# A wider column pitch for the split activations of a decoder-layer kernel, with small tiles placed in the gaps

## What is computed

```python
x = x + 0.5 * swiglu_ffn(x, ffn1_norm, ffn1_w_in, ffn1_w_out)   # 1024 -> 2 x 2816 -> 1024
h = rmsnorm(x, mix_norm); proj = h @ w_in                        # 1024 -> 2048: u, q, k, v, q_mem
y = concat(pool_mixer(u), moba_attention(q, k, v), mem_attention(q_mem))
x = x + y @ w_out                                                # 1024 -> 1024
x = x + 0.5 * swiglu_ffn(x, ffn2_norm, ffn2_w_in, ffn2_w_out)
```

## Time and profile before

| | us |
|---|---|
| median of 3 runs | 561.92 (560.6 to 562.0) |
| the profiled execution's own time | 560.33 |
| its span, first to last instruction | 558.5 |
| PE busy | 551.9 (99%) |
| DVE busy | 398.8 (71%) |
| ACT busy | 269.4 (48%) |

### The profile page before, as it was taken

The page is one execution under the profiler, slowest core; times in us unless marked ns, Lnnn a source line. Parts: engine busy times, 40 slices in busy tenths (PEclk is TensorE's granted clock), DMA queues, the critical chain, the costliest instruction groups (busy, mean ns, idle before and its releaser), DMA issues.

```text
span 558.5 us, 13391 instructions
## 1 busy us (share of the span) xinstructions
PE 551.9 (99%) x5075; PEld 514.3 (92%) x5075; DVE 398.8 (71%) x715; ACT 269.4 (48%) x425; POOL 17.7 (3%) x24
## 2 busy tenths in 40 slices
PE   9999999999999999999999999999999999999997
PEld 9999999999899998566777779999999999999997
DVE  4686878885688877899936685689777777664444
ACT  6843465444543337344535885475444344433330
POOL 1000000000000003000000000140000000000000
PEclk9999999999999999999999999999999999999999
DMA  8799999784567664899999984567756666465523
GB/s 242 220 262 303 268 316 282 239 248 152 191 217 273 209 205 154 283 344 383 361 315 377 374 301 137 164 179 196 211 171 188 186 171 191 133 226 181 188 75 79
DMA packets 137480, 128.40 MB, mean 230 GB/s; under 512 B 10936, under 2 KB 108879, under 8 KB 137431
## 3 DMA queue, kind: packets, MB, share of 16 engines
q1 hardware_dynamic: 134703, 127.24, 72.6%
q10 hardware_dynamic: 2736, 0.61, 0.5%
HBM read 125.12 MB, written 2.83 MB: 229 GB/s over the span
## 4 chain that ended last, share of the span: by engine, by line
PE 83%; DVE 7%; DMA 5%; ACT 2%; issue 1%; SPq 1%; DVEq 0%; ACTq 0%
PE banks L1506 24%; PE banks L1507 24%; PE banks L1508 24%; DMA raw<-in_ffn_w_in 4%; PE banks L1666 3%; PE banks L1514 2%; PE banks L1940 2%; DVE w_lo L1022 2%; PE banks L1638 1%; PE banks L1867 1%; PE banks L1891 1%; DMA page_ids<-in_page_table 1%; DVE banks L1436 0%; DVE kp L1138 0%; ACT w_hi L702 0%
## 5 line engine op out<-in xcount | busy, mean ns | idle before, releaser
L702 ACT ACTIVATE w_hi<-raw 128x1024 fp32r<-128x1024 f32 x158 | 166.4, 1058 | 195.7 <-PE banks L1508 157.6
L1022 DVE TENSOR_TENSOR w_lo<-raw,w_hi 128x1024 fp32r<-128x1024 f32 x158 | 193.8, 1232 | 74.2 <-ACT w_hi L702 73.2
L1506 PE MATMUL banks<-x_hi,w_hi 128*128 128x264 f32 x752 | 214.1, 285 | 0.2 <-DVE h_tmp L1066 0.2
L1507 PE MATMUL banks<-x_lo,w_hi 128*128 128x264 f32 x752 | 213.0, 283 | 0.0
L1508 PE MATMUL banks<-x_hi,w_lo 128*128 128x264 f32 x752 | 213.0, 283 | 0.0
L1506 PEld LDWEIGHTS banks<-x_hi,w_hi 128*128 128x128 f32 x752 | 141.6, 188 | 0.8 <-issue 0.7
L1507 PEld LDWEIGHTS banks<-x_lo,w_hi 128*128 128x128 f32 x752 | 141.7, 188 | 0.0
L1508 PEld LDWEIGHTS banks<-x_hi,w_lo 128*128 128x128 f32 x752 | 141.0, 188 | 0.0
L1506 PE MATMUL banks<-h_hi,w_hi 128*128 (+1 forms) x352 | 100.2, 285 | 0.1
L1508 PE MATMUL banks<-h_hi,w_lo 128*128 (+1 forms) x352 | 100.1, 284 | 0.0
L1507 PE MATMUL banks<-h_lo,w_hi 128*128 (+1 forms) x352 | 100.0, 284 | 0.0
(11 more groups left out here) (287 smaller groups left out, 503.9 us busy)
## 6 DMA issues: line engine op xcount, KB each, us to landing
raw<-in_ffn_w_in SPq DMA_DIRECT2D x86, 512.0 KB, 4.8
raw<-in_ffn_w_out SPq DMA_DIRECT2D x44, 512.0 KB, 3.8
kv<-in_cache_k SPq DMA_DIRECT2D x56, 256.0 KB, 4.9
kv<-in_cache_v SPq DMA_DIRECT2D x48, 256.0 KB, 6.3
raw<-in_w_in SPq DMA_DIRECT2D x12, 512.0 KB, 5.7
late_slot<-in_cache_v SPq DMA_DIRECT2D x16, 256.0 KB, 5.3
raw<-in_w_out SPq DMA_DIRECT2D x8, 512.0 KB, 7.2
raw<-in_mem_w_kv SPq DMA_DIRECT2D x4, 512.0 KB, 3.5
```

The source lines that it names most:

```text
L702: act.activation(w_hi[:, n % RING, :], raw[:, n % RING, :], ACT.Copy).then_inc(hi_ready, 1)
L1022: vec.tensor_tensor(w_lo[:, n % RING, :], raw[:, n % RING, :], w_hi[:, n % RING, :].bitcast(F32), ALU.subtract).then_inc(lo_ready, 1)
L1506: pe.matmul(out, lhs[0], rhs[0], start=start, stop=False)
L1507: pe.matmul(out, lhs[0], rhs[1], start=False, stop=False)
```

## The change

Chunks of `x_hi` and `x_lo` now lie `PITCH` = 288 columns (1,152 bytes) apart, of which 264 are used as before. Between the end of a chunk and the next chunk 96 bytes are free; twelve small tiles move into the last 64 bytes of twelve of these sixteen gaps (`between`), and no longer stand in the row of tiles behind. No instruction is added, removed or moved, and the order of the work is the same; only addresses differ, and the step from chunk to chunk in the instructions that span several chunks.

```diff
+PITCH = 288
...
-        x_hi = place("x_hi", [P, KT, N], F32R)
-        x_lo = place("x_lo", [P, KT, N], F32R)
+        gaps = [cursor[0] + 4 * PITCH * (i + 1) - 64 for i in range(2 * KT)]
+        x_hi = place("x_hi", [P, KT, PITCH], F32R)[:, :, 0:N]
+        x_lo = place("x_lo", [P, KT, PITCH], F32R)[:, :, 0:N]
+
+        def between(name, shape):
+            assert 4 * int(np.prod(shape[1:])) <= 64
+            return place(name, shape, at=gaps.pop(0))
+
...
-        ms = place("ms", [P, 2])
+        ms = between("ms", [P, 2])
...
-        x_rstd = place("x_rstd", [P, 3])
+        x_rstd = between("x_rstd", [P, 3])
...
-        ss_h = place("ss_h", [P, 16])
+        ss_h = between("ss_h", [P, 16])
...
-        rs_h = place("rs_h", [P, 16])
-        mx = place("mx", [P, 4, 2])
-        nb = place("nb", [P, 4, 2])
+        rs_h = between("rs_h", [P, 16])
+        mx = between("mx", [P, 4, 2])
+        nb = between("nb", [P, 4, 2])
```

More of the change, by code:

```diff
@@ L169, in layer @@
         dummy = place("dummy", [P, 4])
-        ms = place("ms", [P, 2])
[L171 to L176, removed]
-        x_rstd = place("x_rstd", [P, 3])
+        ms = between("ms", [P, 2])
+        m_root = between("m_root", [P, 2])
+        m_rstd = between("m_rstd", [P, 2])
+        t_root = between("t_root", [P, 3])
+        t_rstd = between("t_rstd", [P, 3])
+        x_ss = between("x_ss", [P, 3])
+        x_root = between("x_root", [P, 3])
+        x_rstd = between("x_rstd", [P, 3])
         page_ids = place("page_ids", [1, NS * PAGES], I32)
```

## The result

| us | before | after |
|---|---|---|
| median of 13 runs each | 560.75 (559.98 to 562.0) | 562.54 (561.68 to 563.54) |
| span of the profiled execution | 558.5 | 561.0 |
| PE busy | 551.9 | 554.0 |

The change makes the kernel slower: ratio 1.0026, 95% interval 1.0017 to 1.0034, which on 560.75 us is 1.5 us (1.0 to 1.9). A ratio of 1 lies outside that interval, so the loss is clear of the noise, though just short of 0.3%. The forecast was 1.6 us less, so the sign was wrong. The time itself, 562.54 us, is inside the range of 558.2 to 564.2, but that speaks for the rival whose price set its upper end, and not for the forecast. The range also stands on a base of 561.92 us from three runs, where 13 runs give 560.75.

What follows compares the result with a forecast made beforehand. PE, busy 99% at full clock, was taken as the bound through the pace of its matmul triples. 640 triples at 2.5 ns less gave 1.6 us, all other terms 0: 561.92 - 1.6 = 560.3 us, range 558.2 to 564.2.

Steps and rivals of the forecast that it cites:

- the count of 80: Units counted as changing pace: 28 of FFN1, 8 of the mixer output, 44 of FFN2; about 640 triples.
- the test of its mechanism: h's FFN output units stay as before to 0.01 us; a change in them would show the mechanism wrong.
- I take 0.360: FFN input and mixer output triples go from 0.3625 to 0.360 us, 1.6 us less over 640 triples.
- What differs is which bytes move: Triples of one shape and clock have different paces, so pace depends on the address, by up to 3%.
- slower: FFN input units: two remainders 128 apart may be bad; 0.3656 us a triple, 564.0 us; at 0.368, 565.9; chance 0.20.
- PE is late after a wait in the start-up: Near 56.75 us PE starts 0.32 us late after a transfer and h_tmp; expected still late after the change.
- the early units: FFN1's first 16 units (128 triples), set by transfers: faster PE only waits longer, slower PE has 0.32 us of cover.
- The projection: Mixer input projection, x stationary, 192 matmuls: taken as 0, with ends of 1.0 us either way.
- the small tiles: Tiles moved partly into gaps keep instructions and shapes; DVE has 27 us idle in the FFN stage: 0.
- the wider steps of the attention outputs: Attention outputs into x_hi and x_lo step 1,152 bytes instead of 1,056, same instruction count: 0.
- More than that: 0.360 may not be the floor: one matmul per triple gains 5 ns, 3.2 us in all, 558.7 us; chance 0.13.
- No change: FFN units: moving from chunk to chunk costs as before, pace near 0.3625 us a triple, 561.9 us; chance 0.22.

Runs made afterwards that it cites:

- pitch 272: Kernel before with the chunks of x_hi and x_lo 272 columns apart, no small tile moved: 562.24 us in one run.
- 96 bytes in FFN1 and FFN2: Kernel after with 96 free bytes between w_lo and xT, moving all activations against the weights: 564.71 us, ratio to before 1.0069.
- the one with 64 bytes: Kernel after with 64 free bytes between w_lo and xT, moving all activations against the weights: 561.65 us, ratio to before 1.0015.
- The kernel with x_two: Kernel after with x_hi and x_lo of each chunk side by side, x_hi at remainder 128, x_lo at 0: 564.14 us beside 562.26.
- the one with spread slices: Kernel before with FFN input weight slices 136 columns apart, so every chunk has the same distance to its slice: 560.7 us beside 560.74, ratio 0.9993.

## Why the prediction failed

**The bound, the place and the count held.** PE stayed the bound at full clock, no wait came in, no transfer grew into the chain. The 0.02 us came on FFN input units, in 65 of the 72 from 58 us on: 65 x 0.02 = 1.3 us beside a measured 1.5. The mixer output's eight units, which the count of 80 includes, add nothing together. h's units stayed as they were, which the prediction had set as the test of its mechanism; the test was passed though the mechanism was wrong, for by the distance to the weights h stays as well.

**The step that failed** is "I take 0.360", for the pace of a triple, of the two ends 0.360 and 0.368; the units after ran at 2.920 / 8 = 0.365 us. It rested on a sentence ahead of it, "What differs is which bytes move", read as the chunk's remainder alone. Two things were wrong in it. The remainder that counts is that of the distance to the weights. In the earlier trace rows slices always begin at one remainder, so the rows could not show this; it would not have changed the sum, but x and h at like remainders have like distances too, and still differ in pace. For, second, a distance has no one pace. The earlier trace rows are units in which one chunk moves eight times, units in which chunk and slice change with every triple. The after kernel's units hold chunks of 0.36 and of 0.37 us at the same distance, and chunks 5 and 7 of its mixer output differ by 0.06 us in eight triples.

**The evidence against 0.360 was at hand.** The earlier trace rows gave 0.371 and 0.365 at the same two remainders., two chunks in turn, gave 0.3656, and the units came out at 0.365. The prediction called these a rival at 0.20, and chose the rows that shared the tile's name over those that shared the pattern of access. That rival, "slower", had the place and the sign right, and what would show it, units of 2.92 to 2.95 us with no wait on another engine, is what came; its price of 0.3656 was 0.6 ns a triple above what was measured, and its reason, that the two remainders are the bad ones, is only half right: at the same pair of distances 0.360 is seen as well.

**The terms at nothing.** PE is late after a wait in the start-up as before, now 42.83 - 42.27 = 0.56 us against the usual 0.12, instead of the earlier trace rows's place; what the early units cost can't be told from how the transfers happened to arrive. The projection, the small tiles and the wider steps of the attention outputs show no cost that can be told from the 0.35 us that attention adds. In the projection's term the 394 ns of the earlier trace rows belong to 64 of the 192 matmuls; the 64 at L1506 have records of 438 ns, though the term was put at nothing either way. "More than that" is not seen: the fastest units of any layout here are 2.887 us, and the shortest triple seen inside a unit is 0.356. "No change" rested in part on the Trainium skill's "SBUF — State Buffer", section "Who interferes with whom", by which TensorE reads its two operands through independent ports and waits on nobody. That addresses then matter nothing was the prediction's own step, and the runs disagree with it: one unit of 24 matmuls at one clock takes 2.887 to 2.960 us by where its operands lie and what ran ahead of it.

**What stays open.** Why the distance matters was not shown; that reads of moving values and of weights meet in the memory is an argument from the runs with shifted weights, no more. Why the distances 0 and 128 in turn settle at 0.365 us a triple, and not at the 0.360 that both can have, is open too. What selects between two paces of one layout (pitch 272 across the transposes, 96 bytes in FFN1 and FFN2) is unknown. So are the periods. The kernel after has a period of four triples, and its distances modulo 256 are only two; modulo 512 they would be four, but the one with 64 bytes, where they are four as well, has a period of two. The kernel with x_two and the one with spread slices have periods of five and three, though every triple has the same distances modulo 256. The addresses of a unit come round every eight triples, so something besides them must be carried on from matmul to matmul there.

## What to carry to other kernels

Where PE is the bound and every matmul brings its own weight load, a layout can cost or give one or two percent of the matmuls' time with no wait in the profile (2.887 to 2.960 us a unit here): measure it as the start-to-start pace of a repeating unit, not by the time of the whole kernel, which scatters more. Price a layout from rows that have the same access pattern as the place in question (moving operand and weights both changing as they do there), and take the distance between the two operands as the variable. Expect the result to move by as much again with what runs ahead (2.907 and 2.960 us in one layout), so try a few offsets in multiples of 32 bytes and keep the one that measures best; here none beat the old layout by what can be told.

## What was not expected of the hardware

- The pattern of paces follows the distance between moving operand and weights modulo 256: moving the weight rings by 128 bytes turned it by four chunks of 32 bytes, in FFN input and FFN output units alike (h chunks 2 and 6: 2.96 and 2.92 us became 2.92 and 2.96).
- One layout can run at more than one pace in one execution: 2.907 and 2.947 us a unit on either side of some transposes, 2.907 in FFN1 and 2.960 in FFN2, and the same order of chunks at 2.93 and 2.90 from unit to unit.
- A pace, once taken, is stable: 39 units of FFN2 in the kernel after repeat 2.920 us to about 1 ns.
- Triples that lie alike modulo 256 still cycle through several paces, with periods of five (358 to 370 ns) and three (358 to 365 ns) that have nothing to do with the eight chunks of a unit.
- In the kernels whose units all take their chunks in one order, the mean units stand on a grid: 2,886.7, 2,900.0, 2,906.7, 2,913.3, 2,920.0, 2,926.7, 2,933.3, 2,946.7 and 2,960.0 ns are all multiples of 6.67 ns, which is 16 cycles at the granted 2.4 GHz. Of these kernels only the one with x_two (2,922.7) and FFN2 with spread slices (2,904.5) lie between. Why is not known.
